# A recurrent block's kernel: the chunk inverse of the scan by two series, feature edges in one operand, semaphores cleared by ranges

## The reference

```python
def centred_token_shift(u, mu):
    up = centred_pad(u)
    return u + (0.5 * (up[:, :-2] + up[:, 2:]) - u) * mu

def rwkv_features(u, w0, w_up, a0, a_up, k_k, k_a):
    r, k, v, dw_f, dw_b, da_f, da_b = split_cols(u, RWKV_SPLITS)
    kk = to_heads(k * k_k, RWKV_HEADS)
    kk = kk * lax.rsqrt(jnp.sum(kk * kk, axis=-1, keepdims=True) + 1e-12)
    for d, (dw, da) in enumerate(((dw_f, da_f), (dw_b, da_b))):
        w_log = -jax.nn.softplus(-(w0[d] + jnp.tanh(dw) @ w_up[d])) - 0.5
        decay = jnp.exp(-jnp.exp(w_log))
        a = jax.nn.sigmoid(a0[d] + da @ a_up[d])
        k_d = k * (1 + (a - 1) * k_a)
...
    def step(s, inp):                      # wkv_scan, both directions, 8 heads of 64 x 64
        r_t, w_t, k_t, v_t, kk_t, b_t = inp
        sa = jnp.einsum('bhij,bhj->bhi', s, kk_t)
        s = s * w_t[:, :, None, :] - sa[..., None] * b_t[:, :, None, :] + v_t[..., None] * k_t[:, :, None, :]
        y = jnp.einsum('bhij,bhj->bhi', s, r_t) if emit else None
```

## Time and profile before

| | |
|---|---|
| time, median of 3 runs | 4892.66 us (4892.28 to 4894.64) |
| profiled execution | 4893.54 us, span 4891.8 us |
| busy in the span | PE 4407.4 us (90%), PEld 3688.0, DVE 2218.2, ACT 1479.0, POOL 897.0 |
| mean granted clock of PE | 0.94 of full speed |
| feature stage | 1743 to 1930 us |
| scan stage | 1930 to 2881 us |

### The profile page before, as it was taken

The page is one execution under the profiler, slowest core; times in us unless marked ns, Lnnn a source line. Parts: engine busy times, 40 slices in busy tenths (PEclk is TensorE's granted clock), DMA queues, the critical chain, the costliest instruction groups (busy, mean ns, idle before and its releaser), DMA issues. The chain is left out here.

```text
span 4891.8 us, 66510 instructions
## 1 busy us (share of the span) xinstructions
PE 4407.4 (90%) x25709; PEld 3688.0 (75%) x25709; DVE 2218.2 (45%) x3933; ACT 1479.0 (30%) x3174; POOL 897.0 (18%) x852
## 2 busy tenths in 40 slices
PE   8999797998899987999999977998797887999998
PEld 2789786987799843999999953445696666888786
DVE  3224474334421236667777755456412554111134
ACT  2111354655411124222222224002412454122133
POOL 0000452111001923434444434000000000000000
PEclk9999898999999977999999988999898999999999
DMA  7233442103323745111111122023224222111121
GB/s 309 72 114 107 99 85 49 25 23 135 104 89 120 239 163 205 27 27 38 40 47 46 32 92 99 26 99 133 98 92 151 72 94 87 52 47 47 39 86 69
DMA packets 290758, 438.06 MB, mean 90 GB/s; under 512 B 76820, under 2 KB 210550, under 8 KB 285921
## 3 DMA queue, kind: packets, MB, share of 16 engines
q1 hardware_dynamic: 290186, 429.14, 27.7%
q10 hardware_dynamic: 288, 5.07, 0.3%
HBM read 315.09 MB, written 124.03 MB: 90 GB/s over the span
## 5 line engine op out<-in xcount | busy, mean ns | idle before, releaser
L383 PE MATMUL g_acc<-g_wh,l_x_high 128*128 128x320 f32 (+5 forms) x1824 | 593.7, 325 | 46.3 <-DVE g_wl L53 39.6
L383 PE MATMUL g_acc<-g_wh,l_x_low 128*128 128x320 f32 (+5 forms) x1824 | 591.4, 324 | 0.0
L383 PE MATMUL g_acc<-g_wl,l_x_high 128*128 128x320 f32 (+5 forms) x1824 | 591.3, 324 | 0.0
L1546 POOL TENSOR_TENSOR scan_X<-scan_GA,scan_masks 64x256 f32<-64x256 f32 x480 | 362.1, 754 | 233.3 <-ACT scan_GA L1474 198.7
L383 PEld LDWEIGHTS g_acc<-g_wh,l_x_high 128*128 128x128 f32 x1824 | 347.5, 190 | 54.7 <-DVE g_wl L53 41.0
L383 PEld LDWEIGHTS g_acc<-g_wl,l_x_high 128*128 128x128 f32 x1824 | 348.1, 191 | 2.8
L383 PEld LDWEIGHTS g_acc<-g_wh,l_x_low 128*128 128x128 f32 x1824 | 347.2, 190 | 2.4
L431 DVE COPY g_o<-g_acc 128x320 f32<-128x320 f32 (+6 forms) x120 | 62.7, 524 | 577.7 <-PE g_acc L383 540.8
L407 ACT COPY g_o<-g_acc 128x320 f32<-128x320 f32 (+6 forms) x120 | 54.6, 455 | 773.2 <-PE g_acc L383 737.1
L2988 PE MATMUL ffi_acc<-l4a_x_high,ffi_wh 128*128 128x512 f32 x704 | 274.7, 390 | 14.5 <-DVE ffi_wl L53 14.5
L2988 PE MATMUL ffi_acc<-l4a_x_low,ffi_wh 128*128 128x512 f32 x704 | 274.6, 390 | 0.0
(11 more groups left out here) (488 smaller groups left out, 9983.0 us busy)
## 6 DMA issues: line engine op xcount, KB each, us to landing
scan_F<-s_FE SPq DMA_DIRECT2D x160, 192.0 KB, 3.8
s_FE<-feat_f SPq DMA_DIRECT2D x10, 2304.0 KB, 7.8
ffi_w<-in_w_ffn_in SPq DMA_DIRECT2D x44, 512.0 KB, 3.8
g_cu<-s_U SPq DMA_DIRECT2D x24, 768.0 KB, 5.1
pj_o<-s_O SPq DMA_DIRECT2D x26, 512.0 KB, 4.6
front_w<-in_attn_ada_w SPq DMA_DIRECT2D x8, 1536.0 KB, 12.7
front_w<-in_rec_ada_w SPq DMA_DIRECT2D x8, 1536.0 KB, 12.9
g_wr<-in_w_ffn_out SPq DMA_DIRECT2D x44, 256.0 KB, 2.7
```

Source lines behind the costliest of these rows:

```text
L383: mm = pe.matmul(acc[r][:, 0:it["n"]], left, right, start=(k == 0 and q == 0), stop=(k == kt - 1 and q == 2))
L1546: pool.tensor_tensor(X[d][HALF[b], l, :, HALF[b]], GA[d][HALF[b], :, :], lev(d, l)[HALF[b], :].unsqueeze(1).to_broadcast([C, NP2, C]), ALU ...
```

## The change

Three parts, and one reordering.

1. `Stage.clear` sorts the numbers of its semaphores and clears each run of consecutive ones with one instruction.
2. Feature stage: the edge rows of all ten tiles are loaded once (40 partitions), split into an fp32r high part and a remainder in the same 40 rows, and multiplied by a `ends` matrix of each tile, in fp32r (one pass). The low-rank inputs and `wup` are split in the same way into fp32r operands (POOL: `lows`; four copies of 32 rows). f gets three buffers. `begin` also makes two operands kp from k and k_a, and `finish` makes k_d as z * kp0 + kp1. Waits for constants are placed where each is first used. ACT takes the low-rank inputs of the next tile before it writes out the present one.
3. Scan: the inverse is formed by products of powers of a near part (16 x 16 blocks) and then of the far part, in seven steps with one product each per direction; steps 2, 3 and 6 multiply a power and the running sum together (`MR`, 128 columns). The second Gram matrix and `turn(n, 3)` stand between the steps. The second triangular product is dropped: its exponential becomes exp(-F3) * exp(sum), with the product by POOL (`shift`). The second KB copy goes to ACT, `decay` is folded into `state`. POOL's masked matrices are three, over 128 partitions.
4. Hyena filters: SP waits for the small operands before `load_y`, the second window comes before the second `load_y`, and DVE's wait for `cst` comes after the first tile's taps.

The diff, cut to its core:

```diff
     def clear(self):
-        for s in self.sems:
-            self.nc.sync.sem_clear(s)
+        ids = sorted(s.num for s in self.sems)
+        first = 0
+        for i in range(1, len(ids) + 1):
+            if i == len(ids) or ids[i] != ids[i - 1] + 1:
+                self.nc.sync.sem_clear(range(ids[first], ids[i - 1] + 1))
+                first = i
         self.nc.all_engine_barrier()
...
-        edge = [st.sb(f"edge{b}", [2, RW]) for b in range(3)]
+        edge = st.sb("edge", [4 * NT, RW])
+        edge_hi = st.sb("edge_hi", [4 * NT, RW], F32R)
+        edge_two = st.sb("edge_two", [4 * NT, RW], F32R)
-        f = [st.sb(f"f{b}", [P, 2, NF * 4, HD]) for b in range(2)]
+        f = [st.sb(f"f{b}", [P, 2, NF * 4, HD]) for b in range(3)]
...
+                sp.dma_start(shift[:, :], ap["shift"]).then_inc(shift_in, 16)
+                for half in range(2):
+                    for j in range(2):
+                        to = (2 * half + j) * NT
+                        for tiles, row0, out0 in segments:
+                            sp.dma_start(edge[to:to + tiles, :], ...).then_inc(edge_in, 16)
+                            to += tiles
+                sp.dma_start(ends_in[:, :, :], ap["shift_ends"]).then_inc(shift_in, 16)
                 load(0)
...
-                        sp.dma_start(wup[r:r + 32, m, :], ap[wn][0, d]).then_inc(const_in, 16)
-                        sp.dma_start(wup[r + 32:r + 33, m, :], ap[bn][0, d].unsqueeze(0)).then_inc(const_in, 16)
+                        for r in (0, 64, 96):
+                            sp.dma_start(wup[r:r + 32, m, :], ap[wn][0, d]).then_inc(const_in, 16)
+                        sp.dma_start(wup[32:34, m, :], ap[bn][0, d].partition_broadcast(2)).then_inc(const_in, 16)
...
+                def lows(n):
+                    pool.wait_ge(tanh, n + 1)
+                    high(pool, lora_hi[:, :, :], lora[:, :, 0:32]).then_inc(lora_high, 1)
+                    pool.wait_ge(lora_high, n + 1)
+                    low(pool, lora[:, :, 96:128], lora[:, :, 0:32], lora_hi[:, :, :]).then_inc(lora_out, 1)
...
-                        pe.matmul(ps[:, to], shift[:, :], u[n % 3][:, to], start=True, stop=False)
-                        mm = pe.matmul(ps[:, to], ends[:, :], edge[n % 3][:, to], start=False, stop=True)
+                    for to in parts:
+                        pe.matmul(ps[:, to], shift[:, :], u[n % 3][:, to], start=True, stop=False)
+                    if n == 0:
+                        pe.wait_ge(ends_out, 1)
+                        pe.wait_ge(edge_out, 1)
+                    for to in parts:
+                        mm = pe.matmul(ps[:, to], ends[:, n, :], edge_two[:, to], start=False, stop=True)
...
-                    if n >= 2:
-                        dve.wait_ge(stored[b], 16 * (n // 2))
+                    if n >= 3:
+                        dve.wait_ge(stored[n % 3], 16 * (n // 3))
                     dve.tensor_tensor(field(n, 2), split(s[b][:, 512:1024]), split(kk_row[:, :]), ALU.mult).then_inc(kk_raw, 1)
+                    link(dve.tensor_tensor(kp[b][:, 0, :], s[b][:, 512:1024], ka_row[:, :], ALU.mult))
+                    link(dve.tensor_tensor(kp[b][:, 1, :], s[b][:, 512:1024], kp[b][:, 0, :], ALU.subtract))
...
+                    link(dve.tensor_tensor(tmp[:, :, :], z[b][:, 2:4, :], kp[b][:, 0:1, :].to_broadcast([P, 2, HW]), ALU.mult))
                     for d in range(2):
-                        link(dve.scalar_tensor_tensor(out=tmp[:, d, :], in0=z[b][:, 2 + d, :], scalar=-1.0, in1=ka_row[:, :], op0=ALU.add, op1=ALU.mult))
-                    for d in range(2):
-                        for q in range(2):
-                            ins = dve.scalar_tensor_tensor(...)
+                        ins = dve.tensor_tensor(field(n, 4 + 3 * d), split(tmp[:, d, :]), split(kp[b][:, 1, :]), ALU.add)
```

```diff
+                pieces = {1: ((0, 0),), 3: ((0, 1), (0, 2)), 5: ((0, 3),), 6: ((1, 0), (1, 1), (1, 2), (1, 3))}
...
+                def step(n, k):
+                    for d in range(2):
+                        s = e[d]
+                        pe.wait_ge(s["ready"], 8 * n + k)
+                        if k == 1:
+                            pe.wait_ge(s["kb_out"], n + 1)
+                            pe.wait_ge(s["parts"], 4 * n + 3)
+                        if k == 5:
+                            pe.wait_ge(s["parts"], 4 * n + 4)
+                        for h in range(NP2):
+                            if k in (2, 3, 6):
+                                mm = pe.matmul(bank[d][1][:, h * P:(h + 1) * P], SS[d][:, h, :], MR[d][:, h, :, :].rearrange("p x t -> p (x t)"), start=True, stop=True)
+                            else:
+                                of = {1: mid[d][:, h, :], 5: far[d][:, h, :]}.get(k, MR[d][:, h, 1, :])
+                                mm = pe.matmul(bank[d][1][:, h * C:(h + 1) * C], (SX if k == STEPS else SS)[d][:, h, :], of, start=True, stop=True)
+                        mm.then_inc(s["step_mm"], 1)
...
-                        turn(n, 3)
-                        grams(n)
+                        gram(n, 1)
                     if n:
                         mix_s(n - 1)
+                    for k in range(1, STEPS + 1):
+                        if n < NCH:
+                            step(n, k)
+                            if k == 1:
+                                turn(n, 3)
+                            if k == 2:
+                                gram(n, 0)
+                        for d, h in pieces.get(k, ()):
+                            if n and emits(n - 1):
+                                mix_y(n - 1, d, h)
+                            else:
+                                warm(n, d, h)
+                        if k in (4, 5):
+                            if n + 1 < NCH:
+                                sums(n + 1, k - 4)
...
+                def power(n, k):
+                    for d in range(2):
+                        act.wait_ge(e[d]["step_mm"], STEPS * n + k)
+                        nc.scalar.copy(MR[d][:, :, 0, :], single(d) if k in (1, 5) else joint(d)[:, :, 0, :]).then_inc(e[d]["power"], 1)
...
+                def after(n, k):
+                    for d in range(2):
+                        s, R = e[d], MR[d][:, :, 1, :]
+                        if k in (1, 2, 3, 5, 6):
+                            dve.wait_ge(s["power"], 5 * n + {1: 1, 2: 2, 3: 3, 5: 4, 6: 5}[k])
+                            if k < 5:
+                                turned(d, MR[d][:, :, 0, :])
+                            else:
+                                quarters(d, k)
+                            if k in (2, 3, 6):
+                                link[d](dve.tensor_tensor(R, R, joint(d)[:, :, 1, :], ALU.add if k == 3 else ALU.subtract))
+                        elif k == 4:
+                            dve.wait_ge(s["step_mm"], STEPS * n + k)
+                            link[d](dve.tensor_tensor(R, R, single(d), ALU.add))
+                            turned(d, R)
+                        else:
+                            dve.wait_ge(s["step_mm"], STEPS * n + k)
...
+                            for b in range(2):
+                                ins = dve.tensor_tensor(TT[d][n % 2][HALF[b], :, HALF[b]], MR[d][HALF[b], :, 1, :], single(d)[HALF[b]], ALU.add)
...
+                        prepared(d)
...
                     if n < NCH:
                         masked(n, 1)
+                        scaled(n, 3)
+                        for k in range(1, STEPS + 1):
+                            after(n, k)
+                            if k == 2:
+                                masked(n, 0)
                         if n + 1 < NCH:
-                            scaled(n + 1, 3)
+                            for x in range(3):
+                                scaled(n + 1, x)
```

More of the change, by code:

```diff
@@ L1079, in _, with inputs @@
             def _(act):
-                for n in range(NT):
+                def inputs(n):
                     b = n % 2
@@ L1224, in rwkv_scan_stage @@
         e = [{n: st.sem(f"{n}{d}") for n in (
[L1225 to L1226 removed]
+            "loaded0_", "loaded1_", "loaded2_", "blocks", "sums", "exps", "scaled", "turned", "a_out", "kb_out", "kb_late", "grams", "ga", "masked", "parts", "shifted",
+            "step_mm", "power", "ready", "w_mm", "w_out", "u_mm", "u_out", "s_mm", "ys_mm", "y_out", "s_out", "stored0_", "stored1_", "seq")} for d in range(2)]
         FEv = FE.rearrange("(n c) b f -> n c b f", c=C)
@@ L1690, in scan_constants @@
     masks = [s < t, s <= t, s > t, s >= t]
-    for before in (True, False):
-        for n in range(6):
-            b = 1 << n
-            same = (s // (2 * b)) == (t // (2 * b))
-            masks.append(same & (s // b < t // b if before else s // b > t // b))
+    pair, near = s // 2 == t // 2, s // 16 == t // 16
+    for m in (s < t, s > t):
+        masks += [pair & m, near & ~pair & m, ~near & m]
     return tri, np.ascontiguousarray(np.stack(masks, 1).astype(f))
```

(7 more changed lines are left out.)

347 lines of the change are left out of this document (183 added, 164 removed).

## The result

| | before | after |
|---|---|---|
| time, median | 4892.47 us (4 runs, 4889.8 to 4894.64) | 4979.19 us (4 runs, 4972.6 to 4989.27) |
| ratio | | 1.0179, 95% interval 1.016 to 1.0198 |
| profiled execution, its span | 4893.54, 4891.8 us | 4972.6, 4970.8 us |

The change makes the kernel 1.8% slower. The forecast was 4859, its range ended at 4925, and slower had a chance of 0.15.

A forecast was written before the change was run, and what follows sets the result against it. TensorE was taken to set the scan's pace, the store plus VectorE work the feature stage's. 4893.5 - 29 (clears) - 31 (feature stage) + 28 (scan) - 2 (Hyena opening) = 4859.5, less 0.9: 4859 us; range 4785 to 4925.

The forecast's parts named there:

- Clears, -29: All stage ends: 553 single semaphore clears become one or two range clears per stage, saving 29 us.
- Feature stage, -31: Feature stage: earlier start saves 14 us and a shorter period per tile 17 us.
- the term for GpSimd: Feature stage, per tile: 1.4 us added because VectorE's new operations run beside GpSimd's two products.
- The product: Feature stage, per tile: VectorE's new product of 1024 elements was put at 1.35 us.
- Hyena opening, -2: Hyena filters' start: VectorE begins some 4 us sooner, GpSimd waits for a later load_y; net -2 us.
- Scan, prologue, -3: Scan, ahead of the first start: ten fewer memsets save 3 us.
- Scan, the walk: One output chunk followed in written order: period 45.2 us (+-1.5), with VectorE's queue late next; 48.3 with warm-up products.
- Scan, the clock: Scan: TensorE's idles lower the granted clock, adding 1.0 us per chunk (bounds 0 and 5).
- The clock stays low, slower: Rival, scan: idle before turn(n, 3) costs each chunk 10 us at half clock; +109 us, 4940 in all; chance 0.13.
- what would show it: List of expected signs; for the scan, period 45 to 47 us, VectorE busy over 80%, clock below 0.98.
- over 48 (clock): Sign in the scan: a chunk period over 48 us would show the forecast wrong because of the clock.
- 6.3 us of relief for TensorE: Scan, per chunk: fewer product instructions save 5.4 us, the dropped triangular product 0.9; all expected to turn into idle.

The follow-up runs named there:

- clears_only: The kernel before the change, with only the clears by ranges added; 4861.43 us, ratio 0.9954.
- fill_more: Changed kernel plus unread TensorE products: 13 ahead of turn(n, 3), 10 ahead of step 4, 3 between its directions, 3 ahead of step 5, 5 within step 6; 4870.55 us.
- fill_rest: Changed kernel plus 21 unread TensorE products at steps 4 to 6, none ahead of turn(n, 3); 4909.67 us, ratio 1.0028.
- old_scan: Changed kernel with the scan stage and scan constants of the kernel before; 4847.7 us, ratio 0.9903.
- old_one_warm: Against old_scan, warm-up products cut from 6 to 1 in each of 8 places of the first five chunks; 4876.88 us, ratio 0.9992.
- fill_both: Changed kernel plus unread TensorE products, 13 ahead of turn(n, 3) and 6 ahead of step 4; 4922.84 us, ratio 1.0062.
- old_fill: Against old_scan, 2 unread TensorE products added ahead of each direction of level_p(n, 2); 4843.42 us, ratio 0.9905.

## Why the prediction was wrong, point by point

- **Clears, -29: right.** 553 became 43; in clears_only, where 40 are left, they gave 32 us alone.
- **Feature stage, -31: right, -36.5 with 1.2 of clears in it.** The stage's first DMA went out at 1729.90, 13.5 us sooner than in the earlier trace rows's trace; from it the first sigmoid came 17.4 us sooner than before (forecast 14). The period fell from 13.7 to 11.7 us (forecast 11.8; tiles in the middle of the stage take 12.05). Inside, the term for GpSimd was short: the two sums take 3.3 us where I had 1.44 and 1.4 for interference. The product was a little long, 1.22 us for 1.35.
- **Hyena opening, -2: too small, -8.5 with 1.8 of clears in it.** VectorE starts 9.6 us after the stage does, where the earlier trace rows had the end of a 17.12 us wait, and GpSimd's later start (21.4 us in, 18.3 before) did not undo the gain.
- **Scan, prologue, -3: right.** From the stage's start to the first copy of scan_GA 26.5 became 23.5.
- **Scan, the walk: right in its marks and its length, but not in who is busy.** With 0 at the start of `mix_w` (2528.80 less a period, 2474.26), every mark down to the first low stretch lies within 0.5 us: copy of GA ends at 10.8 (10.55), step 1 at 14.7 to 16.7 (14.65 to 16.45), `turn(n, 3)` at 19.7 (19.3). With the clock held, in fill_more, step 4 starts at 30.9 (30.4) and step 7 at 44.7 (43.6), and an output chunk takes 46.5 us, at the upper end of the walk's 45.2 +- 1.5 and with the added products in it. But "VectorE stays at some 37.5 us per chunk, and now owns the longer work" rests on prices that hold the gaps between instructions (1.06 us for a pair of transposes that lasts 0.91). The profile has VectorE busy 33.8 us in an output chunk, 73% of fill_more's 46.5, and TensorE's own work is about 38 (an estimate: 45.5 busy, less 34 added products of 0.223). Neither fills the chunk; at full clock it is as long as the chain that passes through both and ScalarE.
- **Scan, the clock: this step failed.** "I add 1.0 (bounds 0 and 5)." Held against fill_more it cost 8.1 us in an output chunk, and in the first chunks 2.7 over before, where 0.8 was forecast. I had taken the 3.4 us behind one gap of 2.1 us in another stage as the price of an idle; here 6.8 us followed the first idle and 17 the second, smaller one, and while they lasted they nearly doubled the time of the products on the chain, steps 5 and 6 among them. The argument that "the idle that TensorE now has takes part of it" did not hold: of the 17.0 us TensorE is busy 16.7, so there is no idle to take it.
- **The rival was the right one, and under-sized too.** *The clock stays low, slower* named the idle ahead of `turn(n, 3)` and gave it 10 us at half clock and 4940. The idle is enough to start it (fill_rest), but by itself it makes 6.8 us; the rest comes with the idles at step 4 (it goes when they are filled too, in fill_more), which the rival left out. 24 us at half clock go with 4979. The chance of 0.13 rested on "half a chunk's low stretches fall where VectorE leads", which no row showed.
- **Of what would show it**: the last sentence had it right, "over 48 (clock)". VectorE's busy share in an output chunk went from 77% to 62%, not over 80%. The 80% could not have come true even at the forecast's own period: 33.8 us of 46.2 are 73%.

The place of the error is a habit of the sum: 6.3 us of relief for TensorE were booked as worth nothing, because they became idle. With the clock lost by that idle they were worth less than nothing.

## What to carry to other kernels

When a change takes work off an engine that was 96% busy, ask what its clock does before asking what bounds next; walk the chain twice, once with every TensorE product at half clock behind each idle, and let the second walk be the range's upper end. Short idles can count as well as a long one. Once the chain is the bound, real work moved into TensorE's idles, and a few products that nothing reads where none is left, turned a loss of 87 us into a gain of 102.

## What the runs showed of the hardware

- Less work made the kernel slower, 4876.9 us against old_scan's 4847.7: 8.9 us of TensorE's work taken out of each of five chunks made four of them 62 to 66 us long instead of 48 to 53, at half clock for 44 to 55 us of them (old_one_warm).
- Two idles of 0.66 and 0.43 us were followed by 13.7 us at 1.2 GHz in nearly all output chunks (fill_both); one of 3.07 us, with no other over 0.25, by 6.8 (fill_rest). It is not a law: idles of 1.19 and 0.44 us were followed by full clock once and by half clock another time in the same execution (old_one_warm).
- In the old scan, TensorE 98% busy, single stretches of 34 to 48 us at half clock appear in some executions and not in others and cost about 20 us. Filling two idles did not end them (old_fill), and their cause is open. "In some executions" is read from the times and mean clocks; the stretch itself was seen in three profiles, one each of clears_only, old_scan and old_fill. In the versions whose chunks held full clock none appeared in the profiled executions.
